# Reordered steps, a mask product on another engine and a shared sum row in a two-layer decoder step

## What is computed

```python
# mLSTM, one head, chunkwise form; b is the running sum of the log forget gates
w = exp(dmat - m_t)                                  # decay weights
s = (q @ k.T) * w
num = s @ v + a * (q @ C)                            # numerator
den = s.sum(-1) + a * (q @ n)
h = num / maximum(abs(den), exp(-m_t))               # then gated by sigmoid(o)
C_new = ae * C + sum_s ws[s] * outer(k[s], v[s])     # new matrix memory, per request
n_new = ae * n + sum_s ws[s] * k[s]                  # new normaliser
# attention on the prompt, one head
p = softmax(q @ k.T * scale - slope * distance, causal)
o = p @ v
```

## Time and profile before

| what | us |
|---|---|
| median of three runs | 936.86 |
| the runs | 935.07, 936.86, 937.08 |
| profiled execution, its own time | 935.07 |
| its span, first to last instruction | 933.2 |
| PE busy (share of the span) | 917.1 (98%) |
| DVE busy | 626.6 (67%) |
| ACT busy | 437.3 (47%) |
| POOL busy | 45.6 (5%) |
| mean granted TensorE clock | 0.993 of full speed |

### The profile page before, as it was taken

One profiled execution on the slowest core, in us unless ns is written; L12 is line 12 of the kernel. 1 busy time (PEld: TensorE's weight loads), 2 busy tenths in 40 slices (PEclk: granted clock), 3 DMA queues, 4 the chain that ended last, 5 costly groups with the idle time before them and its releaser, 6 DMA issues.

```text
span 933.2 us, 19004 instructions
## 1 busy us (share of the span) xinstructions
PE 917.1 (98%) x7618; PEld 854.2 (92%) x7618; DVE 626.6 (67%) x1118; ACT 437.3 (47%) x816; POOL 45.6 (5%) x61
## 2 busy tenths in 40 slices
PE   9999999999999999999999999999999999999996
PEld 8999888899999999998888779877999999999994
DVE  6577568778976575775676747454568797657555
ACT  5445656466355363544443552443446634536321
POOL 0000002400000000410000000000220000000000
PEclk9999999999999999999999999999999999999998
DMA  9972215654454444557887997999945455444301
GB/s 287 271 222 91 91 46 136 193 180 137 136 171 145 136 159 157 172 182 264 289 282 261 345 358 301 393 370 359 281 137 180 136 180 182 136 140 167 101 1 57
DMA packets 134224, 182.79 MB, mean 196 GB/s; under 512 B 5845, under 2 KB 116125, under 8 KB 134136
## 3 DMA queue, kind: packets, MB, share of 16 engines
q1 hardware_dynamic: 128750, 177.29, 57.5%
q10 hardware_dynamic: 4746, 2.18, 0.9%
q0 software_dynamic: 640, 2.10, 0.8%
HBM read 175.23 MB, written 6.32 MB: 195 GB/s over the span
## 4 chain that ended last, share of the span: by engine, by line
PE 93%; DMA 3%; DVE 1%; SPq 1%; ACT 1%; issue 0%; ACTq 0%; DVEq 0%; POOL 0%; POOLq 0%
PE ps L550 24%; PE ps L552 24%; PE ps L551 24%; PE ps L888 6%; PE ps L930 3%; DMA page<-in_cache_v_dram 3%; PE ps L986 2%; PE ps L565 1%; PE ps L583 1%; SPq L479 0%; SPq L482 0%; PE ps L669 0%; PE ps L736 0%; PE ps L971 0%; PE ps L649 0%
## 5 line engine op out<-in xcount | busy, mean ns | idle before, releaser
L1086 ACT ACTIVATE w_hi<-raw 128x1024 fp32r<-128x1024 f32 x192 | 202.7, 1058 | 247.6 <-PE ps L552 239.2
L1470 DVE TENSOR_TENSOR w_lo<-raw,w_hi 128x1024 fp32r<-128x1024 f32 x192 | 234.8, 1224 | 111.4 <-ACT w_hi L1086 111.2
L550 PE MATMUL ps<-x_hi,w_hi 128*128 128x322 f32 (+1 forms) x888 | 279.4, 315 | 0.1
L552 PE MATMUL ps<-x_hi,w_lo 128*128 128x322 f32 (+1 forms) x888 | 276.3, 311 | 0.0
L551 PE MATMUL ps<-x_lo,w_hi 128*128 128x322 f32 (+1 forms) x888 | 276.0, 311 | 0.0
L550 PE MATMUL ps<-h_hi,w_hi 128*128 128x320 f32 x632 | 196.7, 311 | 0.5 <-DVE h_lo L1608 0.5
L552 PE MATMUL ps<-h_hi,w_lo 128*128 128x320 f32 x632 | 195.0, 309 | 0.0
L551 PE MATMUL ps<-h_lo,w_hi 128*128 128x320 f32 x632 | 195.0, 309 | 0.0
L550 PEld LDWEIGHTS ps<-x_hi,w_hi 128*128 128x128 f32 x888 | 168.0, 189 | 5.4 <-ACT k_turned L1368 3.1
L551 PEld LDWEIGHTS ps<-x_lo,w_hi 128*128 128x128 f32 x888 | 168.5, 190 | 0.2
L552 PEld LDWEIGHTS ps<-x_hi,w_lo 128*128 128x128 f32 x888 | 167.5, 189 | 0.0
(11 more groups left out here) (352 smaller groups left out, 902.4 us busy)
## 6 DMA issues: line engine op xcount, KB each, us to landing
raw<-in_w_up_dram SPq DMA_DIRECT2D x32, 1024.0 KB, 5.7
raw<-in_w_down_dram SPq DMA_DIRECT2D x32, 1024.0 KB, 5.1
page<-in_cache_k_dram SPq DMA_DIRECT2D x64, 512.0 KB, 5.2
page<-in_cache_v_dram SPq DMA_DIRECT2D x64, 512.0 KB, 6.5
raw<-in_w_in_a_dram SPq DMA_DIRECT2D x12, 1024.0 KB, 9.4
raw<-in_w_kv_dram SPq DMA_DIRECT2D x8, 1024.0 KB, 7.2
raw<-in_w_out_a_dram SPq DMA_DIRECT2D x4, 1024.0 KB, 5.2
raw<-in_w_q_b_dram SPq DMA_DIRECT2D x4, 1024.0 KB, 5.1
```

What stands on the lines that cost most here:

```text
L550: mm(out, WH[t % SPL][:, k, :], hi[:, k, 0:width], start=(k == 0), stop=False)
L552: last = mm(out, WL[t % SPL][:, k, :], hi[:, k, 0:width], start=False, stop=(k == 7))
L1086: A(WH[t % SPL][:, :, :], raw[RBUF[u]][:, :, 128 * (t % 2):128 * (t % 2) + 128], ACT.Copy)\
L1470: V.tensor_tensor(WL[t % SPL][:, :, :], raw[RBUF[t // 2]][:, :, 128 * (t % 2):128 * (t % 2) + 128], WH[t % SPL][:, :, :].bitcast(F32), ALU ...
```

## The change

Eight edits, none of them changes a result:

1. DVE no longer runs `decay` one head ahead: `decay(h)` stands directly in front of `weights(h)`.
2. ACT does `v_copy(7)` after `normalised(6)` instead of in front of it.
3. DVE does `state(0)` in front of `gated(7)` and `h_rest(7)`.
4. v_masked is made by POOL, in eight products of 64 x 512, in front of its running sums; ACT's sixteen instructions go. The semaphore now counts heads, so PE waits for 2j + 2.
5. The two prompt halves of the normaliser sum go to the same PSUM row as one accumulation. DVE's two instructions that copied and added rows go; ACT copies the one row, in `prompt_state_out`, and the DMA of the prompt's normaliser moves there.
6. ACT does `p_exp(i)` first in each attention step, in front of the two copies.
7. ACT does `out_copy(0, ...)` after step 3 instead of after step 4.
8. DVE does `head_low(i-2)` last in a step, behind `p_norm(i)` and behind whatever `reciprocals`, `scale_out` and `out_low` stand there, instead of in front of `p_norm(i)`.

```diff
@@ -726,7 +726,7 @@
                     j = n - 2
                     pe.wait_ge(s_wk, 8)
                     pe.wait_ge(s_hg, H)
-                    pe.wait_ge(s_vm, j + 1)
+                    pe.wait_ge(s_vm, 2 * j + 2)
                     for half in range(2):
                         if j >= 2:
                             pe.wait_ge(s_cadd, 2 * j - 3 + half)
@@ -762,10 +762,9 @@
                     for q in range(2):
                         mm(o, wsK[:, q, 64 * h:64 * h + 64], VT[:, q, h, 0:128],
                            start=(q == 0), stop=(q == 1), skip_group_check=True)
-                mm(ps[5][0:1, :], ones[:, 0:1], wsK[:, 0, :], start=True, stop=True, skip_group_check=True)
-                mm(ps[5][64:65, :], ones[:, 0:1], wsK[:, 1, :], start=True, stop=True, skip_group_check=True)
-                mm(ps[5][32:40, :], bmask[0:64, :], wsK[0:64, 2, :], start=True, stop=True, skip_group_check=True)\
-                    .then_inc(s_np, 1)
+                for q in range(2):
+                    mm(ps[5][0:1, :], ones[:, 0:1], wsK[:, q, :], start=(q == 0), stop=(q == 1))
+                mm(ps[5][32:40, :], bmask[0:64, :], wsK[0:64, 2, :], start=True, stop=True).then_inc(s_np, 1)
 
             def ln_stats(l):
 
@@ -1194,8 +1193,8 @@
                     normalised(h - 2)
                 if h >= 3:
                     h_rounded(h - 3)
+            normalised(6)
             v_copy(7)
-            normalised(6)
             h_rounded(5)
             normalised(7)
             h_rounded(6)
@@ -1209,16 +1208,6 @@
             def gain_bias(l):
                 A(XH[:, :, T:TW], lnrow(lnT, l), ACT.Copy).then_inc(s_gbh, 1)
 
-            def masked(j):
-
-                if j == 0:
-                    act.wait_ge(s_hg, H)
-                    act.wait_ge(s_vc, 8)
-                for b in range(4):
-                    ins = A(Vm[:, 2 * j:2 * j + 2, b, :], VT[0:64, 2, 2 * j:2 * j + 2, 0:128], ACT.Copy,
-                            scale=bmask4[0:64, b:b + 1])
-                ins.then_inc(s_vm, 1)
-
             def x_rounded(l, n):
 
                 act.wait_ge(s_xr, 8 * l + n + 1)
@@ -1238,11 +1227,13 @@
 
             def prompt_state_out():
                 act.wait_ge(s_np, 1)
+                A(npr[:, :], ps[5][0:1, :], ACT.Copy)
                 A(Wst[:, :], ps[4][:, :], ACT.Copy).then_inc(s_nadd, 1)
                 act.wait_ge(s_nadd, 1)
                 for h2 in range(2):
                     act.dma_start(p_C[0, 0].rearrange("(j t) k v -> t k j v", t=2)[h2],
                                   Wst[64 * h2:64 * h2 + 64, :].rearrange("p (j v) -> p j v", j=4)).then_inc(s_po, 16)
+                act.dma_start(p_n[0, 0].rearrange("h k -> (h k)").unsqueeze(0), npr[:, :]).then_inc(s_po, 16)
 
             def mlp(l, q0, hl0):
 
@@ -1265,9 +1256,7 @@
                             if l == 0 and i == 0 and n == 4:
                                 prompt_state_out()
                             if l == 0 and i == 1 and n == 4:
-                                act.wait_ge(s_nout, 2)
-                                act.dma_start(p_n[0, 0].rearrange("h k -> (h k)").unsqueeze(0), npr[:, :])\
-                                    .then_inc(s_po, 16)
+                                act.wait_ge(s_nout, 1)
                                 act.dma_start(s_n[0].rearrange("b h k -> b (h k)"), nout[:, :]).then_inc(s_po, 16)
                         else:
                             split_to(t + 4)
@@ -1288,8 +1277,6 @@
                     gain_bias(0)
                 x_rounded(0, n)
                 squared(0, n)
-                if n < 4:
-                    masked(n)
                 if n == 1:
                     act.wait_ge(s_nm, 1)
                     store(p_m[0, 0:1, :].rearrange("a h -> h a"), mnew[:, 0:1])
@@ -1342,13 +1329,13 @@
                 A(PTt[h % 2][:, :], ps[3][:, 0:384], ACT.Copy).then_inc(s_pTc, 1)
 
             def p_step(i):
+                if 0 <= i < H:
+                    p_exp(i)
                 if 0 <= i - 2 < H:
                     act.wait_ge(s_pV, i - 2 + 1)
                     A(HH[0][:, i - 2, 0:TP], ps[0][:, 0:256], ACT.Copy).then_inc(s_xhp, 1)
                 if 0 <= i - 1 < H:
                     p_copy(i - 1)
-                if 0 <= i < H:
-                    p_exp(i)
 
             def q_lay(G):
 
@@ -1429,7 +1416,7 @@
             probs_copy(1)
             for i in range(H + 2):
                 p_step(i)
-                if i == 4:
+                if i == 3:
                     out_copy(0, 0)
                     out_copy(0, 1)
             out_copy(1, 0)
@@ -1608,10 +1595,8 @@
                 V.tensor_tensor(HL[0][:, h, :], hg[h % 2][:, :], HH[0][:, h, :].bitcast(F32), ALU.subtract)\
                     .then_inc(s_hl, 1)
 
-            decay(0)
             for h in range(H):
-                if h + 1 < H:
-                    decay(h + 1)
+                decay(h)
                 weights(h)
                 split(8 * Q_V + h + 3)
                 if h >= 2:
@@ -1670,9 +1655,9 @@
                                                          c_bank(j, half)[:, 128 * bb:128 * bb + 128], ALU.mult, ALU.add)
                         ins.then_inc(s_cadd, 1)
 
+            state(0)
             gated(7)
             h_rest(7)
-            state(0)
             for n in range(8):
                 t = 8 * Q_WOA + n
                 residual(0, t, ALPHA)
@@ -1766,8 +1751,6 @@
                                             ALU.subtract).then_inc(s_hl, 1)
                             if l == 0 and i == 1 and n == 0:
                                 dve.wait_ge(s_np, 1)
-                                own(V.tensor_copy(npr[:, :], ps[5][64:65, :]))
-                                V.tensor_tensor(npr[:, :], npr[:, :], ps[5][0:1, :], ALU.add).then_inc(s_nout, 1)
                                 own(V.tensor_tensor(nout[:, :].rearrange("p (h k) -> p h k", h=8),
                                                     n0[:, :].rearrange("p (h k) -> p h k", h=8),
                                                     bcast(cols[0:8, 48:56], 2, DK), ALU.mult))
@@ -1844,8 +1827,6 @@
             def p_step(i):
                 if 0 <= i < H:
                     p_max(i)
-                if i >= 2:
-                    head_low(i - 2)
                 if 0 <= i < H:
                     p_norm(i)
 
@@ -2007,6 +1988,8 @@
                 if i == 8:
                     reciprocals(1)
                     scale_out(1, 0)
+                if i >= 2:
+                    head_low(i - 2)
             scale_out(1, 1)
             out_low(1, 0)
             out_low(1, 1)
@@ -2063,6 +2046,11 @@
                 ins = G.tensor_copy(aqZ[:, :, b, 8 * (b % 4):8 * (b % 4) + 8], aqT[:, :, 8 * b:8 * b + 8])
             ins.then_inc(s_aqz, 1)
 
+            pool.wait_ge(s_hg, H)
+            pool.wait_ge(s_vc, 8)
+            for h in range(H):
+                G.tensor_tensor(Vm[:, h, :, :], bcast(VT[0:64, 2, h, 0:128], 1, 4),
+                                bcast(bmask4[0:64, :], 2, 128), ALU.mult).then_inc(s_vm, 1)
             for n in range(1, 7):
                 sums(0, n)
             for j in range(4):
```

## The result

| | before | after |
|---|---|---|
| median of the runs, us | 936.97 (4 runs) | 944.87 (4 runs) |
| the runs, us | 935.07 to 937.57 | 944.09 to 947.1 |
| ratio after / before | | 1.0097 (95%: 1.008 to 1.0114) |
| profiled execution, its own time | 935.07 | 946.36 |
| mean granted TensorE clock in it | 0.993 | 0.991 |

The changed kernel is slower. The medians differ by 7.9 us. The 21 executions of after that were recorded have a mean of 945.8 us, and the ratio, which takes them all in, gives 9.1 us (7.5 to 10.7). The prediction was +5.85. The profiled execution of after is 11.3 us longer than that of before.

What follows compares the result with a forecast made beforehand. PE, busy for 917.1 of 933.2 us, was taken to bound the kernel. The terms 1.15 + 1.5 + 0.7 + 0.85 + 1.65 = 5.85, on the median of 936.86, gave 942.7 us, with a range of 939.2 to 946.0.

Steps and rivals of the forecast that it cites:

- all seven places at which PE was to wait longer: Expected PE waits: third `scores` on weights, last `numerator` on v_tok, h_lo at the output projection, `p_out` at four heads.
- third `scores`: At `scores(2)`, PE waits for DVE's weights because decay lost its one-head lead: +1.15 us.
- last `numerator`: At `numerator(7)`, PE waits because ACT's `v_copy(7)` now follows `normalised(6)`: +1.5 us, bounds 1.3 to 1.6.
- sum row: Prompt normaliser sum: four matmul pieces follow one another instead of running side by side: +0.85 us, bounds 0 and 1.2.
- four `p_out`: Attention steps: `p_out` at heads 1, 3, 4 and 6 waits, +0.5, +1.25, +0.5, +1.05, together 3.3 us.
- v_masked on POOL: 0: Memory products: POOL's products, estimated at 1.4 to 2.1 us each, are ready before PE wants them, costing 0.
- POOL is late: Rival: v_masked products at 3 us each make PE wait and hold up ACT's weight splits; 946 to 951 us, chance 0.08.
- `state(0)`: Output projection's first tile: scaled keys ahead of `gated(7)` delay h_lo, for which PE waits: +0.7 us, bounds 0 and 1.1.
- The page waits: End of the attention stretch: PE's existing 1.6 us wait for pages absorbs that much of the `p_out` delays.
- net of the attention steps: Attention steps: the 3.3 us of `p_out` delays less 1.6 us of page-wait cover, +1.65 us, bounds 0.5 and 3.5.
- Mostly covered: Rival: waits at `scores(2)`, attention and normaliser sum mostly vanish; +2 to +2.5 us, 937 to 939, or no change; chance 0.10.
- faster: Rival: ACT's exponentials first shorten the attention chain by up to 8 times 0.8 = 6.4 us; near 935 us, chance 0.04.

Runs made afterwards that it cites:

- mask_one_input: The kernel before, with v_masked made by POOL in 16 instructions of 64 x 256 with a per-partition scalar: 942.83 us, ratio 1.0062.
- mask_back_on_act: The changed kernel with only the v_masked move undone, so ACT makes it again: 942.85 us, ratio 1.0063 against before.
- attention_edits: The kernel before with only the three reorderings of ACT and DVE in the attention steps (edits 6, 7, 8): 938.14 us, ratio 1.0021.
- after_early_state: The changed kernel with all eight edits, plus DVE making the second pair of scaled keys right behind the first residual: 942.79 us, ratio 1.0068 against before.
- state_first: The kernel before with edit 3 alone, `state(0)` in front of `gated(7)`: 937.45 us, ratio 1.0014.
- decay_and_copy: The kernel before with edits 1 and 2 alone, decay without its lead and the later `v_copy(7)`: 938.61 us, ratio 1.0026.
- mask_on_pool: The kernel before with edit 4 alone, v_masked made by POOL in eight products: 939.54 us, ratio 1.0027.
- shared_sum_row: The kernel before with edit 5 alone, one accumulated PSUM row for the prompt's normaliser: 936.24 us, ratio 1.0005.

## Why the prediction was right or wrong

**Direction and places.** Slower was right (0.90), and all seven places at which PE was to wait longer show it. The terms for the third `scores` (1.15; measured 1.07), the last `numerator` (1.5; 1.5), the sum row (0.85; 0.85 to 0.87) and the four `p_out` (3.3; 3.4) stand within 0.2. They were worked out from the distances of starts and from the instruction in front of which the moved one was put, in the earlier trace rows.

**The step that failed** is the term "v_masked on POOL: 0". It asked whether POOL would be in time for PE (it was, at 1.16 a product) and priced nothing on the third engine. Measured alone, edit 4 costs +0.43 at h_lo, +1.31 at wsk, and what the clock takes behind it: 3.0 in the mean of twelve runs. The sum gave the right sign of the danger, 1307 against 881 for the same running sum, and read it as POOL's own slowness. It was POOL waiting for DVE: that sum, of 166.94, ran into the x_lo of 166.95 to 167.50. The same lock in the other direction stretches DVE, and the trace of before held this too, from 382 to 401, where the running sums of a later layer norm (one at 381.79) fall beside x_lo:

```profile
382.07 1.17 DVE L1643 SCALAR_TENSOR_TENSOR x_lo<-x,ln_cols,x_hi 128x320 fp32r<-128x320 f32 x1
```

This x_lo takes 0.55 where POOL is idle. With that row the question "what does DVE lose, and who waits behind it?" could have been asked before any run. The chance of 0.08 for "POOL is late" was set for another mechanism, though mask_one_input shows that this one exists too, once POOL takes over 15 us.

**`state(0)`** was right: +0.7, measured +0.70 net alone. In after the step is 1.22 less 0.19, since h_lo(7) came under the lock too (0.93 for 0.49); in mask_back_on_act, without the lock, it is 0.71 less 0.24.

**The page waits** were to give back 1.6. From the last `p_out` to the last page they gave 0.8 in after and 0.6 in attention_edits, and only 0.4 in mask_back_on_act and after_early_state. The net of the attention steps up to the last page is therefore +2.6 and +2.8 in the first two, +3.0 in the others (2.3 in the means of attention_edits' runs), and not +1.65. Late releases of pages, which the prediction names before it takes the full 1.6, would explain this, but no run shows them as the cause. PE's waits for pages at this place also change where no edit touches the attention: 1.6 us in before, 2.0 in state_first, 2.4 in decay_and_copy, 2.5 in mask_on_pool, 2.6 in shared_sum_row. A difference of some 1 us between two executions can be chance.

**The sum.** By the differences of the means the pieces are 2.4 (edits 1, 2) + 1.2 (3) + 3.0 (4) + 0.6 (5) + 2.3 (6 to 8) = 9.5, against 9.1 (7.5 to 10.7) for the whole change. The intervals are 1.0 to 1.7 us to either side for each piece, so this shows no large gain or loss between the edits, and could not show one of 2 us. Of the 3.3 by which 9.1 exceeds 5.85, edit 4 holds 3.0 by its runs (0.9 to 4.2). The other side of the account agrees: all edits but 4 have a mean of 943.3, close to the 942.7 that the sum gave with nothing for edit 4. The rest of the misses are about 1 or less each. The range's upper end, 946.0, left POOL's contention out of the bounds (its terms add up to 945.4, and those of the low end to 939.8, not 939.2); with 936.97 x 1.0097 = 946.1 the result lies just above that end.

**Rivals.** "Mostly covered" and "faster" are out. The mechanism of "faster", exponentials first, is not just too small: with edit 7, and without 8, it makes the kernel 1.3 slower in the mean (0.1 to 2.3). No kernel here beats before.

## What to carry to other kernels

When work moves to an engine that is idle, ask not only whether that engine is in time, but which instructions of the others share something with it, and what is queued behind *these*. Here that meant sorting DVE's instructions by what they read (two SBUF tensors, or one and PSUM) and looking for the first one that PE waits for behind a blocked one. The list of waits isn't enough for this: a wait of part of a group of matmuls stands inside PE's busy row, and shows only as a row that is longer than its like. And two reorderings on two engines can put the same link into the same chain: their costs, each measured alone, then don't add.
